# RWKV inverses: 16x16 diagonal blocks by forward substitution on VectorE beside the projection, passed through DRAM, with two doubling levels left on TensorE

## The reference, cut to what matters

```python
def step(state, inp):
    r_t, w_t, k_t, v_t, a_t, b_t = inp
    sa = jnp.einsum('bhvk,bhk->bhv', state, a_t)
    state = (state * w_t[:, :, None, :] + sa[..., None] * b_t[:, :, None, :]
             + v_t[..., None] * k_t[:, :, None, :])
    return state, jnp.einsum('bhvk,bhk->bhv', state, r_t)
```

## Time and profile before

| | us |
|---|---|
| median of three executions | 2021.36 (2020.91 to 2022.54) |
| the profiled execution: span | 2020.4 |
| setup | 0 to 30 |
| projection, layer 0 and layer 1 | 30 to 194, about 1017 to 1182 |
| chunks, layer 0 and layer 1 | 194 to 306, 1182 to 1294 |
| PE busy over the span | 96% |

### The profile page before, as it was taken

The page is one execution under the profiler, slowest core; times in us unless marked ns, Lnnn a source line. Parts: engine busy times, 40 slices in busy tenths (PEclk is TensorE's granted clock), DMA queues, the critical chain, the costliest instruction groups (busy, mean ns, idle before and its releaser), DMA issues. The chain is left out here.

```text
span 2020.4 us, 27165 instructions
## 1 busy us (share of the span) xinstructions
PE 1939.5 (96%) x11406; PEld 1035.1 (51%) x11406; DVE 651.8 (32%) x1309; ACT 382.6 (19%) x733; POOL 78.9 (4%) x140
## 2 busy tenths in 40 slices
PE   7999999999999999999699999989999999999996
PEld 4446995455444444443254489754554444444443
DVE  7245665225311111111244556451451111111112
ACT  3131325234000000000112232350520000000001
POOL 3001000000000000000200010010000000000001
PEclk9999999999999999999899999999999999999998
DMA  8000001521799999999840000032239999999996
GB/s 354 0 0 1 3 3 50 208 84 42 314 413 428 428 429 427 431 426 429 319 197 0 0 2 3 10 138 113 84 133 412 421 428 427 429 429 428 428 428 241
DMA packets 51547, 481.86 MB, mean 238 GB/s; under 512 B 7216, under 2 KB 12080, under 8 KB 23792
## 3 DMA queue, kind: packets, MB, share of 16 engines
q1 hardware_dynamic: 49136, 471.91, 56.1%
q0 software_dynamic: 2304, 8.39, 1.2%
HBM read 461.14 MB, written 19.14 MB: 238 GB/s over the span
## 5 line engine op out<-in xcount | busy, mean ns | idle before, releaser
L1961 PE MATMUL bank<-ring,hT 128*64 128x512 f32 x2080 | 471.2, 595 | 12.5 <-DVE hT L1992 6.8
L1961 PEld LDWEIGHTS bank<-ring,hT 128*64 128x64 f32 x2080 | 143.2, 137 | 284.7 <-issue 263.9
L1954 PE MATMUL bank<-arena 128*128 128x256 f32 x1088 | 251.9, 385 | 0.9 <-DVE arena L1982 0.9
L904 PE MATMUL bank<-hT,ring 128*128 128x512 f32 (+1 forms) x576 | 249.5, 593 | 0.0
L1968 PE MATMUL bank<-ring,arena 128*64 128x512 f32 x1040 | 236.6, 597 | 5.6 <-DMA ring<-in_we 4.5
L1954 PEld LDWEIGHTS bank<-arena 128*128 128x128 f32 x1088 | 201.4, 190 | 77.6 <-issue 52.8
L904 PEld LDWEIGHTS bank<-hT,ring 128*128 128x128 f32 (+1 forms) x576 | 108.1, 188 | 139.2 <-issue 138.0
L1992 DVE TENSOR_TENSOR hT<-bank,colp 128x512 f32<-128x512 f32 x68 | 47.1, 692 | 395.2 <-PE bank L1954 395.2
L2257 ACT ACTIVATE arena<-bank 128x256 f32<-128x256 f32 x65 | 25.0, 384 | 662.1 <-PE bank L1940 662.1
L1968 PEld LDWEIGHTS bank<-ring,arena 128*64 128x64 f32 x1040 | 70.6, 137 | 143.8 <-issue 136.4
L2409 DVE COPY arena<-bank 128x512 f32<-128x512 f32 x65 | 45.0, 692 | 257.1 <-PE bank L1968 257.1
(11 more groups left out here) (449 smaller groups left out, 2009.9 us busy)
## 6 DMA issues: line engine op xcount, KB each, us to landing
ring<-in_we SPq DMA_DIRECT2D x195, 2048.0 KB, 18.1
expert_rows<-arena SPq DMA_DIRECT2D x130, 128.0 KB, 15.2
ring<-in_w_in SPq DMA_DIRECT2D x6, 2048.0 KB, 19.2
ring<-in_w_out SPq DMA_DIRECT2D x4, 2048.0 KB, 9.7
ring<-in_wm SPq DMA_DIRECT2D x2, 2048.0 KB, 7.8
ring<-in_w_in SPq DMA_DIRECT2D x2, 1920.0 KB, 17.0
ring<-in_w_in SPq DMA_DIRECT2D x2, 1664.0 KB, 27.1
ring<-in_w_in SPq DMA_DIRECT2D x2, 1152.0 KB, 28.9
```

The costliest lines, as they stand in the source:

```text
L904: last = nc.tensor.matmul(B[n % 4][0:w, :], ins_units[unit][:, k, u0:u0 + w], hT[:, k, :], start=k == 0, stop=k == KD - 1)
L1954: last = nc.tensor.matmul(bank[:, o:o + GS], htok[:, i, k * P:(k + 1) * P], selg[z][:, i, :], start=i == 0, stop=i == NT - 1)
L1961: last = nc.tensor.matmul(bank[CAP * j:CAP * j + CAP, :], x[:, k, :], up_w(u, j, k), start=k == 0, stop=k == KD - 1)
```

## The change: what it does

The 16x16 diagonal blocks of all 32 matrices of a layer are inverted during the projection, and the chunks stage is left with the two doubling levels that go from 16 to 32 and from 32 to 64, for blocks (`LEVELS = (3, 4)`), and the join.

- In setup, SP also writes zeros to the 64x64 diagonal halves of a new DRAM tensor `li_d` (two DMAs from a zero tile, through `diagonal_halves`: 64 partitions x 32 matrices x 64 elements each).
- In the projection, DVE computes `BT` right after `X1`. PE computes after the weight tile of place 16 the 64x64 halves of A for all 32 matrices (`early_a`: 64 products). ACT copies them from four banks to `a_half`. SP stores them to a DRAM tensor `am_d` (two DMAs), waits, loads the 256 diagonal blocks of 16x16 back, one block to a partition and half (two DMAs through `diagonal_blocks`: 128 partitions x 16 rows x 16 elements each), waits; POOL masks them and sets the diagonal (two `affine_select`); DVE inverts all 256 at once in 14 steps of two instructions; SP stores the inverses to `li_d` (two DMAs), waits, and issues the load of the halves of the first 16 matrices (`load_starts`, two DMAs). The bonus of the last step of DVE comes after the inversion. PE's `bonus_sums` also waits for the copies.
- In the chunks stage, `start_block` on POOL and DVE is gone; `start_flip` waits for the load instead. SP loads the halves of the other 16 matrices when the join of the first pass is done.

```diff
+        am_d = nc.dram_tensor("decay_products", (NT * RH, P + 1, P), F32, kind="Internal").ap()
+        li_d = nc.dram_tensor("block_inverses", (NT * RH, P + 1, P), F32, kind="Internal").ap()
+        def diagonal_blocks(mat, z):
+            step = 16 * P + 16
+            return bass.AP(mat.tensor, z * P * step, [[step, P], [P, 16], [1, 16]])
+        def diagonal_halves(mat, R, m0, m1):
+            return mat[m0:m1, R, R].rearrange("m i j -> i m j")
...
                 load_w_in(eng, slice(0, 1), (1, 0, 2, 4, 5))
+                eng.wait_ge(s_gc, 1)
+                for R in HALVES:
+                    eng.dma_start(diagonal_halves(li_d, R, 0, NT * RH),
+                                  zero64[R, :].unsqueeze(1).to_broadcast([64, NT * RH, 64])).then_inc(s_lz, 16)
                 eng.wait_ge(s_in, 16 * 2)
...
+            def load_starts(eng, z):
+                for R in HALVES:
+                    eng.dma_start(XLc[R, :, :], diagonal_halves(li_d, R, 2 * RH * z, 2 * RH * z + 2 * RH)
+                                  ).then_inc(s_li[z], 16)
...
                     eng.wait_ge(s_par, 16 * NPAR)
+                    eng.wait_ge(s_eac, NT)
+                    for R in HALVES:
+                        eng.dma_start(diagonal_halves(am_d, R, 0, NT * RH), a_half[R, :, :]).then_inc(s_ao, 16)
+                    eng.wait_ge(s_ao, 32)
+                    eng.wait_ge(s_bp, 1)
+                    for z in range(2):
+                        eng.dma_start(a_blk[:, z, :, :].rearrange("p r c -> p (r c)"),
+                                      diagonal_blocks(am_d, z)).then_inc(s_ai, 16)
+                    if not layer:
+                        eng.wait_ge(s_lz, 32)
+                    eng.wait_ge(s_lb, 1)
+                    for z in range(2):
+                        eng.dma_start(diagonal_blocks(li_d, z),
+                                      l_blk[:, z, :, :].rearrange("p r c -> p (r c)")).then_inc(s_lo, 16)
+                    eng.wait_ge(s_lo, 32)
+                    load_starts(eng, 0)
...
+                    eng.wait_ge(s_bm, 1)
+                    for j in range(1, 15):
+                        left, below = 15 - j, slice(j + 1, 16)
+                        t = blk_t[:, 0:2 * left * j].rearrange("p (z i c) -> p z i c", z=2, i=left)
+                        v(eng.tensor_tensor(t, l_blk[:, :, below, j:j + 1].to_broadcast([P, 2, left, j]),
+                                            l_blk[:, :, j:j + 1, 0:j].to_broadcast([P, 2, left, j]), ALU.mult))
+                        v(eng.tensor_tensor(l_blk[:, :, below, 0:j], l_blk[:, :, below, 0:j], t, ALU.add))
+                    eng.sem_inc(s_lb, 1)
...
+                    def early_a():
+                        eng.wait_ge(s_ab, 1)
+                        for z in range(2):
+                            for m in range(RH):
+                                n, c = 2 * z + m // RC, m % RC
+                                for e in range(2):
+                                    rows = slice(64 * e, 64 * e + 64)
+                                    for R in HALVES:
+                                        tok = slice(n * P + R.start, n * P + R.stop)
+                                        last = nc.tensor.matmul(B[4 + 2 * z + e][R, m * 64:(m + 1) * 64],
+                                                                AT[rows, c, tok], BT[rows, c, tok], start=True,
+                                                                stop=True)
+                            last.then_inc(s_ea, 1)
...
-                    between = {5: lora_a, 6: lora_decay, 10: kk_sums, 11: kk_spread, NTILE + 1: bonus_sums}
+                    between = {5: lora_a, 6: lora_decay, 10: kk_sums, 11: kk_spread, 16: early_a, NTILE + 1: bonus_sums}
...
+            LEVELS = (3, 4)
+            ADDED = 4 * NL + 2
+                @block.sync
+                def _(eng):
+                    eng.wait_ge(s_u1, ADDED)
+                    load_starts(eng, 1)
+                    eng.wait_ge(s_li[1], 32)
...
-                        for L in range(5):
+                        for l, L in enumerate(LEVELS):
...
-                                    eng.wait_ge(s_xi, n0 // 2 + 1)
+                                    eng.wait_ge(s_li[n0 // 2], 32)
                                     start_flip(0).then_inc(s_x0, 1)
-                        eng.wait_ge(s_am, 2 * n0 + 4)
-                        v(start_block(eng, v, 1))
                         start_flip(1).then_inc(s_x0, 1)
```

More of the change, by code:

```diff
@@ L106, in build @@
         s_w1 = ctx.enter_context(nc.semaphore("first_weights_scaled"))
+        s_lz = ctx.enter_context(nc.semaphore("block_inverses_blanked"))
         layer_sems = []
@@ L129, in build @@
         causal = sb("causal", [P, P])
[L130 to L132 removed]
+        lvl = sb("lvl", [P, 2, 32])
+        zero64 = sb("zero64", [P, 64])
         scan_keep = sb("scan_keep", [P, SEQ])
@@ L404, in _ @@
                 fill(epsc[:, 5:6], EPS * EPS)
+                fill(zero64[:, :], 0.0)
                 eng.sem_inc(s_gc, 1)
@@ L421, in _ @@
                 keep(causal[:, :], [[-1, P]], 0, 1, ALU.is_ge, -BIG)
[L423 to L426, removed]
-                for L in range(5):
-                    b = 2 << L
-                    v = wide[:, L, :].rearrange("p (a j) -> p a j", j=b)
+                wide = ring_view(5, 3584, 128).rearrange("p (l t) -> p l t", l=2)
+                fill(wide[:, :, :], 1.0)
+                for l, b in enumerate((16, 32)):
+                    v = wide[:, l, :].rearrange("p (a j) -> p a j", j=b)
                     keep(v, [[-2 * b, 64 // b], [0, b]], 0, 1, ALU.is_ge, 0.0)
                     keep(v, [[2 * b, 64 // b], [0, b]], b, -1, ALU.is_gt, 0.0)
[L432 to L436, removed]
+                for R in HALVES:
+                    g(eng.tensor_copy(lvl[R, :, :], wide[R, :, R.start // 2:R.stop // 2]))
                 fill(head_pick[:, :, :], 0.0)
@@ L735, in _ @@
                     eng.sem_inc(s_b8, 1)
-                    for n in range(16, NTILE):
+                    evict(16)
+                    for z in range(2):
+                        eng.wait_ge(s_ea, z + 1)
+                        for e in range(2):
+                            eng.activation(a_half.rearrange("p (z m e) j -> p z e m j", z=2, e=2)[:, z, e],
+                                           B[4 + 2 * z + e][:, :].rearrange("p (m j) -> p m j", j=64),
+                                           ACT.Copy).then_inc(s_eac, 1)
+                    for n in range(17, NTILE):
                         evict(n)
@@ L977, in quarter @@
                 return ap[:, 4 * q:4 * q + 4, :]
[L979 to L990, removed]
-            with nc.Block() as block:
+            LEVELS = (3, 4)
+            NL = len(LEVELS)
+            ADDED = 4 * NL + 2
+            with nc.Block() as block:
+                @block.sync
[3 more added lines that the diff above has]
+                    eng.wait_ge(s_li[1], 32)
                 @block.tensor
@@ L1059, in _ @@
                         eng.wait_ge(s_gm, RH * n0 + 2 * RH)
-                        for L in range(5):
+                        for l, L in enumerate(LEVELS):
                             for q in range(4):
-                                if L:
-                                    eng.wait_ge(s_xa, levels + 4 * (L - 1) + q + 1)
+                                if l:
+                                    eng.wait_ge(s_xa, levels + 4 * (l - 1) + q + 1)
                                 else:
@@ L1164, in _ @@
                     g = gch.on(eng)
[L1165 to L1173, removed]
-                        eng.wait_ge(s_xi, n0 // 2 + 1)
[L1175 to L1178, removed]
+                    eng.wait_ge(s_bz, 2)
+                    g(eng.memset(XU[0][64:128, :, 0:64], 0.0))
+                    g(eng.memset(XU[1][64:128, :, 0:64], 0.0))
+                    eng.sem_inc(s_xz, 1)
                 @block.scalar
```

48 lines of the change are left out of this document (32 added, 16 removed).

## The result

The changed kernel takes 1996.78 us (median of four executions, 1996.14 to 1997.98) against 2021.45 for the kernel before: ratio 0.987, 95% interval 0.9845 to 0.9894. The forecast was 2001.

What follows compares the result with a forecast made beforehand. PE was taken to bound the projection and chunks stages, with levels on the path. -44.9 + 2 x 4.4 + 14.2 + 1.5 = -20.4 on the span of 2020.4 gave 2000, plus 1.0 carried over: 2001 us, range 1983 to 2048.

Steps and rivals of the forecast that it cites:

- Levels: Chunks stage: three levels removed in two passes of two layers, 12 x 3.74 = 44.9 us saved.
- `early_a`: Projection: 64 added products on PE's path at 58 ns each, 3.7 us, between 1.7 and 7.
- The chain: Projection: store, load, POOL, DVE and store in a row end at 198.3, PE and ACT at 198.0.
- the 20 ns a packet: Projection's DMA chain: 20 ns for every short packet, so each pair of DMAs takes 6.85 us.
- SP held in setup: Setup: blanking DMAs behind w_in hold SP, so layer 0's projection starts at 44.8 instead of 30.6, 14.2 us lost.
- The clock: Start of layer 0's projection: PE's clock is 0.50 for 3.0 us after standing still, costing 1.5 us.
- The blanking holds nobody: Setup: issues are not held by a full queue, so setup costs nothing, 1985 us; chance 0.15.
- Short stores cost double: Setup and projections: stores under 512 B take 56 ns a packet instead of 28, 2047 us; chance 0.15.
- All short pieces at 28 ns: Setup and projections: every short piece costs what 512 B ones do, chain ends at 204.8, 2018 us; chance 0.17.
- the signs that the prediction named as right: Profile after: DMA pairs about 7 us each, chunks stages 4 us later, SP and PE arriving together.

Runs made afterwards that it cites:

- Experiment 7: Changed kernel with blocks of 8x8 and three levels on PE instead of blocks of 16 and two levels: 2010.16 us, ratio 0.9948 to the kernel before.
- experiment 9: Changed kernel with both blanking DMAs in the projection, early_a's 64 products ordered one row half after the other: one execution, span 1983.9 against 1981.3.
- experiment 6: Changed kernel with 28 more multiplications into scratch on DVE behind the inversion: 2007.37 us, ratio 0.9928 to the kernel before.
- experiment 3: Changed kernel with one blanking DMA left in setup, the other issued in the projection of layer 0: 1982.32 us, ratio 0.9805 to the kernel before.
- Experiment 5: Changed kernel with 27, 13 or 15 keep-busy matmuls at the end of PE's setup list: 2003.51, 1995.97 and (one execution) 1994.96 us.
- experiments 1 and 2: Changed kernel with both blanking DMAs moved from setup to layer 0's projection: 1981.7 us; kernel before with only the two blanking DMAs added in setup: 2035.96 us.
- experiment 8: Changed kernel with both blanking DMAs in the projection, blocks of 32x32 and one level on PE: 1993.89 us, ratio 0.9867 to the kernel before.
- experiment 4: Kernel before with groups of extra short and large stores on SP in the projection of layer 0: one execution, 2019.25 us.

## Why the prediction was right, and where its terms were off

The forecast's mechanism is what happened: two levels left, a chain hidden in the projection, SP held in setup, and a low clock behind it. Its sum was -20.4 and the span says -26.0; the time forecast, 2001, is 4.2 us above the measured 1996.78. One row of the kernel before is needed for the first step, the end of the second pass's last level in layer 0:

```profile
282.47 3.79 PE L1085 MATMUL bank<-hT,ring 128*128 128x64 f32 x32
```

By its steps:

- **Levels:** -44.9 put, -45.2 measured (22.93 in layer 0, 22.31 in layer 1). The two layers differ because in layer 0 of before, and not in layer 1, the last two levels of the second pass took 282.47 - 274.35 = 8.12 us and not 7.5. The two that remain take 7.58 (225.23 to 232.81). Why that one pass was 0.6 longer stays open. Experiment 7 gives the price of a level alone.
- **`early_a`:** 3.7 put, 2.10 measured; the wait before it 0.28 (0.4 put). The guess took the 58 ns of a level's products, where two work at a time, and only experiment 9 shows that this was the wrong row for four quarters. PE's stage grew by 2.57 and not by 4.1: together with the next step this is the largest miss, 3.7 us in two layers.
- **The chain:** put at the same length as PE, 198.3 against 198.0; it has 4.4 us to spare (experiment 6: 4.2). The first store was well put (7.2 with its wait, 6.85), DVE too (7.8, 7.6). The load and the second store were not, with 4.75 and 4.5 in place of 6.85: the 20 ns a packet held for 256 B (18.5) but not for 64 B (10.8 and 8.8), where the earlier trace rows had said 10 and I had distrusted it. In the sum this cost only 0.3 a layer, since PE's end was as late.
- **SP held in setup:** 14.2 put, 12.65 measured. The number was near by luck, for the reading behind it was wrong. An issue isn't held for its own packets (experiment 3), but by what is in front of it. The prediction's picture, that of the 258 packets 170 must be gone, would have held the first issue too; it took 0.86 us. Of the first blanking some 54 packets an engine of 129 were done when the second issue ended, by the packets of that stretch, so SP came free 2 us sooner than put.
- **The clock:** 1.5 put, 2.34 measured. The first group of products took 3.55 us to the next one's start where it takes 1.79 at full clock, the second 1.44 where it takes 0.86: +1.76 and +0.58. So both groups ran at the low level or partly at it, longer than the 3.0 us that I took from the earlier trace rows. Experiment 5 puts the whole 2.34 on the clock.

The differences: 0.3 (levels) + 3.66 (projections) + 1.55 (setup) - 0.84 (clock) + 0.9 (in the other stages, not followed) = 5.6, which is what lies between the sum and the span.

The rivals. *The blanking holds nobody* is out: it holds SP for 32.7 us, and 15 us are its price (experiments 1 and 2). *Short stores cost double* is out: 56 ns a packet were its figure, and the stores of the three pairs take 18.5 at most. The rule of the Trainium skill ("DMA: Bandwidth & Descriptors", section Specifications) that stores below 512 B are read, modified and written back shows no price here: a packet of 64 B takes 8.8 ns and one of 256 B 18.5, where one of 512 B took 28. By the byte the short ones are the dearer, 0.14 ns at 64 B and 0.07 at 256 against 0.055 at 512, but none costs as much as a longer one. *All short pieces at 28 ns* is out by the same rows (its chain, as the terms stand, adds up to 204.4 and not 204.8, which would move its time by 0.8 us).

Three of the signs that the prediction named as right did not come: SP and PE don't arrive together at the projection's end (SP waits 4.4 us), only the first DMA pair takes about 7 us, and the chunks stage starts 2.6 us later behind its projection and not 4.

## What to carry to other kernels

A DMA that nobody waits for can still cost its engine's whole wait: issue it where the queue is empty, and above all not as the second of two behind a long row of loads, when its issuer must still reach a stage's end. Here that cost 15 us, and 12.65 of them were a wait of all five engines for SP. Work moved beside another engine is free only up to the slack of its chain, which here was 4.2 to 4.4 us of 168; read the slack from who waits for whom at the stage's end, and pick the largest size (here blocks of 16) that stays below it. The longer waits of PE cost more than themselves here, for its clock was low behind them: 1.3 us more behind a wait of 4.25 (experiment 6), 1.75 behind one of 11.57 (experiment 8), 2.3 behind one of 12.65.

## What the runs showed of the hardware that was not expected

- The first DMA of 2048 pieces was issued on SP's queue in 0.6 to 0.9 us, also with all of `w_in` or a 2 MB store ahead of it, and the issue behind it was then held: 32.7 us in the change, 11.25 in experiment 3, 7.17 in experiment 4. How many packets may be outstanding did not come out as one number.
- The smaller the piece, the cheaper its packet, all the way down: 28 ns at 512 B, 18.5 at 256 B, 10.8 for 64 B loads and 8.8 for 64 B stores.
- Products of 64x64 with 64 columns on all four quarters of the array in turn took 33 ns each, on one row half after the other 54.
